# Expert 0 of a gMLP and mixture-of-experts layer: its gate and up rows laid out as k*128+p, and its first 1024 features gathered in two pieces of 512

## The reference

```python
h = x + chunked_gmlp(rmsnorm(x, norm_mix), w_in, ln_g, ln_b, w_s, b_s, w_out)
hn = rmsnorm(h, norm_ffn)
# router: the best of 4 groups, in it the best 2 of 8 experts, weights from two softmaxes
# for each expert e, over the tokens routed to it (xb: rows of hn):
y = (silu(xb @ w_gate[e]) * (xb @ w_up[e])) @ w_down[e]     # 2048 -> 512 -> 2048
out = rmsnorm(h + sum_of(weight * y), norm_final)
```

## Time and profile before

| what | before |
|---|---|
| time, median of 3 | 1198.08 us |
| time of the profiled execution | 1198.11 us |
| its span in the profile | 1196.4 us |
| TensorE matmul busy | 883.5 us, 74% |
| DMA rate, mean over the span | 385 GB/s |
| chain of waits, by engine | DMA 50%, PE 47% |
| busiest line of the chain on TensorE | L1395, the mixer, 21% |

### The profile page before, as it was taken

The page is one execution under the profiler, slowest core; times in us unless marked ns, Lnnn a source line. Parts: engine busy times, 40 slices in busy tenths (PEclk is TensorE's granted clock), DMA queues, the critical chain, the costliest instruction groups (busy, mean ns, idle before and its releaser), DMA issues.

```text
span 1196.4 us, 17569 instructions
## 1 busy us (share of the span) xinstructions
PE 883.5 (74%) x7809; PEld 501.8 (42%) x7809; DVE 381.3 (32%) x493; ACT 231.6 (19%) x390; POOL 23.0 (2%) x66
## 2 busy tenths in 40 slices
PE   9999999999984666666666666666666666666666
PEld 7888888877431222222223232222222222222222
DVE  5454866545232222222222222222222222222233
ACT  6644655444200000000000000000000000000003
POOL 1200000000200000000000000000000000000000
PEclk9999999999997777778778787878787887878788
DMA  9875567878999999999999999999999999999997
GB/s 291 327 255 193 193 225 245 302 264 315 399 424 433 429 433 429 434 431 433 433 428 433 434 431 432 434 429 434 431 433 432 430 432 435 429 431 435 426 425 334
DMA packets 47686, 460.93 MB, mean 385 GB/s; under 512 B 4025, under 2 KB 4641, under 8 KB 32289
## 3 DMA queue, kind: packets, MB, share of 16 engines
q1 hardware_dynamic: 46704, 457.19, 92.4%
q0 software_dynamic: 864, 3.21, 0.8%
q10 hardware_dynamic: 80, 0.02, 0.0%
HBM read 458.05 MB, written 2.36 MB: 385 GB/s over the span
## 4 chain that ended last, share of the span: by engine, by line
DMA 50%; PE 47%; SPq 1%; ACT 1%; DVE 1%; issue 1%; POOLq 0%; DVEq 0%
DMA high_slots<-in_e_w_up 48%; PE scattered_out L1395 21%; PE bank L1605 12%; PE bank L1703 5%; PE pair L1566 3%; PE scattered_out L1716 1%; PE pair L1574 1%; DMA out_h<-acc 1%; ACT arena L780 1%; SPq L453 0%; DMA h<-in_x 0%; DVE acc L1261 0%; SPq L469 0%; PE pair L1582 0%; PE bank L1502 0%
## 5 line engine op out<-in xcount | busy, mean ns | idle before, releaser
L1199 DVE TENSOR_TENSOR acc<-scattered_out,acc 128x2048 f32<-128x2048 f32 x58 | 132.9, 2292 | 616.9 <-PE scattered_out L1716 616.9
L1605 PE MATMUL bank<-low_slots,arena 128*32 128x256 f32 x2048 | 153.5, 455 | 147.4 <-DMA low_slots<-in_e_w_up 147.0
L1605 PE MATMUL bank<-high_slots,arena 128*32 128x256 f32 x1952 | 146.0, 457 | 138.4 <-DMA high_slots<-in_e_w_up 138.4
L1605 PEld LDWEIGHTS bank<-low_slots,arena 128*32 128x32 f32 x2048 | 83.9, 126 | 218.8 <-issue 188.8
L1605 PEld LDWEIGHTS bank<-high_slots,arena 128*32 128x32 f32 x1952 | 79.6, 127 | 206.3 <-issue 178.7
L893 DVE TENSOR_TENSOR w_lo<-w_raw,w_hi 128x1024 fp32r<-128x1024 f32 x95 | 116.5, 1226 | 113.8 <-ACT w_hi L601 113.4
L601 ACT CAST w_hi<-w_raw 128x1024 fp32r<-128x1024 f32 x95 | 99.9, 1051 | 126.8 <-PE scattered_out L1395 120.7
L1395 PE MATMUL scattered_out<-w_hi,xT_second 128*128 128x512 f32 x376 | 121.4, 394 | 0.2 <-DVE w_lo L893 0.2
L1395 PE MATMUL scattered_out<-w_hi,xT_first 128*128 128x512 f32 x376 | 120.5, 393 | 0.1
L796 ACT COPY arena<-bank 128x256 f32<-128x256 f32 x32 | 11.9, 372 | 547.9 <-PE bank L1605 547.9
L1703 PE MATMUL bank<-down_slots,arena 128*32 128x512 f32 x944 | 107.9, 596 | 0.7 <-DVE arena L1193 0.7
(11 more groups left out here) (271 smaller groups left out, 512.1 us busy)
## 6 DMA issues: line engine op xcount, KB each, us to landing
down_slots<-in_e_w_down SPq DMA_DIRECT2D x26, 4096.0 KB, 21.1
low_slots<-in_e_w_gate SPq DMA_DIRECT2D x13, 4096.0 KB, 30.2
low_slots<-in_e_w_up SPq DMA_DIRECT2D x13, 4096.0 KB, 39.3
high_slots<-in_e_w_gate SPq DMA_DIRECT2D x13, 4096.0 KB, 30.5
high_slots<-in_e_w_up SPq DMA_DIRECT2D x13, 4096.0 KB, 39.7
w_raw<-in_a_w_in SPq DMA_DIRECT2D x64, 512.0 KB, 3.7
w_raw<-in_a_w_out SPq DMA_DIRECT2D x32, 512.0 KB, 5.0
down_slots<-in_e_w_down SPq DMA_DIRECT2D x6, 2048.0 KB, 19.4
```

The costliest lines, as they stand in the source:

```text
L1199: dve.tensor_tensor(acc[:, t, :], OUT[:, :], (acc if e else h)[:, t, :], ALU.add).then_inc(acc_done, 1)
L1605: ins = pe.matmul(GU[c * CAP:(c + 1) * CAP, 0:256], rows_k, gate_columns(rows_of[c // 2][k], c % 2), start=(a == 0 and k == 0), stop=(a == ...
```

## The change

The gate and up chunks of expert 0 are read in another order: partition p holds the rows k*128 + p. A chunk of 2 MB is then 1024 pieces of 2 KB in memory, where it was 128 pieces of 16 KB. In exchange the features of block k are 128 neighbouring columns of `h`. The first half (features 0 to 1023) is gathered as two quarters of 512 features, each with its own place in PSUM, copy, transpose and scaling, and all three waits (`xe_first_ps`, `xe_first`, `xeT_first`) count to two. The second half stays whole. Its features come with a pattern of two runs of 128 columns. ScalarE's first quarter copy stands ahead of the router's exponentials, its second behind them; VectorE's first scaling stands ahead of the reduction of the exponentials. The scaling takes `g_ffn` (the columns k*128+p of `norm_ffn`) in place of `g_rows`.

```diff
-        XE_FIRST, TRX_FIRST = GU[:, 256:512], TRX[:, 256:512]
+        XE_FIRST = (GU[:, 256:384], XE[:, 256:384])
+        TRX_FIRST = (TRX[:, 256:384], TRX[:, 384:512])
...
                 w, a = (e_gate, e_up)[c % 2], c // 2
+                if e == 0:
+                    return w[0, 0].rearrange("(k p) n -> p k n", p=P)[:, 8 * a:8 * a + 8, :]
                 return w[0, e].rearrange("(p a k) n -> a p k n", a=2, k=8)[a]
...
+            act.wait_ge(xe_first_ps, 1)
+            act.copy(xe[:, 0:P], XE_FIRST[0]).then_inc(xe_first, 1)
             for i in range(2):
                 act.wait_ge(exp_in, i + 1)
                 act.activation((g_exp, e21)[i], (g_shifted, d21)[i], ACT.Exp).then_inc(exp_done, 1)
+            act.wait_ge(xe_first_ps, 2)
+            act.copy(xe[:, P:2 * P], XE_FIRST[1]).then_inc(xe_first, 1)
...
+            def scale_first(lo, hi, src, done):
+                g_first = g_ffn[:, KC * lo:KC * hi].rearrange("p (b j) -> p b j", b=hi - lo).unsqueeze(3)
+                dve.tensor_tensor(xeT[:, lo:hi, :, :], src.rearrange("p (b j c) -> p b j c", b=hi - lo, j=NQ),
+                                  g_first.to_broadcast([P, hi - lo, NQ, CAP]), ALU.mult).then_inc(done, 1)
+            dve.wait_ge(exp_in, 2)
+            dve.wait_ge(xeT_first_ps, 1)
+            scale_first(0, 1, TRX_FIRST[0], xeT_first)
             dve.wait_ge(exp_done, 2)
...
             dve.wait_ge(g_rows_in, 16)
-            scale_first(0, xeT_first_ps, TRX_FIRST, xeT_first)
+            dve.wait_ge(xeT_first_ps, 2)
+            scale_first(1, 2, TRX_FIRST[1], xeT_first)
             choose(0)
-            scale_first(1, xeT_ps, TRX, xeT_ready)
+            dve.wait_ge(xeT_ps, 1)
+            scale_first(2, 4, TRX[:, 0:2 * P], xeT_ready)
...
-                for t in range(NT):
-                    ins = gather_first(0, t)
-                ins.then_inc(xe_first_ps, 1)
+                gather_quarter(0, 0)
+                gather_quarter(0, 1).then_inc(xe_first_ps, 1)
+                gather_quarter(1, 0)
                 pe.wait_ge(xe_first, 1)
-                transpose_first(0).then_inc(xeT_first_ps, 1)
-                gather_first(1, 0)
+                transpose_quarter(0).then_inc(xeT_first_ps, 1)
+                gather_quarter(1, 1).then_inc(xe_first_ps, 1)
...
                 pe.wait_ge(xeT_first, 1)
                 gate_up_of(0, 0, rows_of, 0, 2).then_inc(gu_pair, 1)
-                gather_first(1, 1).then_inc(xe_ps, 1)
+                pe.wait_ge(xe_first, 2)
+                transpose_quarter(1).then_inc(xeT_first_ps, 1)
                 gate_up_of(0, 0, rows_of, 2, 4).then_inc(gu_pair, 1)
+                gather_second_half(0)
+                gather_second_half(1).then_inc(xe_ps, 1)
+                pe.wait_ge(xeT_first, 2)
                 gate_up_of(0, 0, rows_of, 4, 8).then_inc(gu_half, 1)
                 pe.wait_ge(xe_ready, 1)
```

More of the change, by code:

```diff
@@ L782, in copy_first @@
             def copy_first():
-                act.wait_ge(xe_first_ps, 1)
-                act.copy(xe[:, 0:2 * P], XE_FIRST[:, 0:2 * P]).then_inc(xe_first, 1)
                 act.wait_ge(xe_ps, 1)
@@ L1175, in _ @@
             g_of = g_rows[:, :].rearrange("p (b k) -> p k b", k=KC).unsqueeze(3).to_broadcast([P, KC, NQ, CAP])
[L1177 to L1184, removed]
             def scale_xeT(e):
@@ L1583, in transpose_scat, with gather_quarter, gather_second_half, transpose_quarter @@
                 ins.then_inc(scat_ps, 1)
-            def gather_first(half, t):
+            def gather_quarter(q, t):
                 pe.wait_ge((sel_first, sel_ready)[t], 1)
                 for j in range(NB):
-                    cols = h[:, t, :].rearrange("q (p a j b) -> q a j p b", a=2, j=NB, b=2)[:, half, j, :, :]
-                    ins = pe.matmul((XE_FIRST, XE)[half][j * CAP:(j + 1) * CAP, 0:2 * P], sel[:, 0, t, :], cols,
+                    col = q * NBLK + j * P
+                    ins = pe.matmul(XE_FIRST[q][j * CAP:(j + 1) * CAP, :], sel[:, 0, t, :], h[:, t, col:col + P],
                                     start=(t == 0), stop=(t == NT - 1))
                 return ins
[L1594 to L1598, removed]
-                return ins
+            def gather_second_half(t):
+                for j in range(NB):
+                    cols = h[:, t, :].rearrange("q (a j p) -> q a j p", a=KC, j=NB)[:, 2:4, j, :]
+                    ins = pe.matmul(XE[j * CAP:(j + 1) * CAP, 0:2 * P].rearrange("c (a p) -> c a p", a=2), sel[:, 0, t, :],
+                                    cols, start=(t == 0), stop=(t == NT - 1))
+                return ins
+            def transpose_quarter(q):
+                return pe.transpose(TRX_FIRST[q], xe[:, q * P:(q + 1) * P], ident[:, :])
             def gate_up_of(e, a, rows_of, lo, hi):
                 for k in range(lo, hi):
-                    rows_k = xeT[:, 2 * a + k % 2, k // 2, :] if e == 0 else xeT[:, k % KC, 2 * a + k // KC, :]
+                    rows_k = xeT[:, 2 * a + k // KC, k % KC, :] if e == 0 else xeT[:, k % KC, 2 * a + k // KC, :]
                     for c in range(NQ):
@@ L1621, in first_expert @@
                 gate_up_of(0, 0, rows_of, 0, 2).then_inc(gu_pair, 1)
-                gather_first(1, 1).then_inc(xe_ps, 1)
+                pe.wait_ge(xe_first, 2)
+                transpose_quarter(1).then_inc(xeT_first_ps, 1)
                 gate_up_of(0, 0, rows_of, 2, 4).then_inc(gu_pair, 1)
+                gather_second_half(0)
+                gather_second_half(1).then_inc(xe_ps, 1)
+                pe.wait_ge(xeT_first, 2)
                 gate_up_of(0, 0, rows_of, 4, 8).then_inc(gu_half, 1)
                 pe.wait_ge(xe_ready, 1)
-                transpose_first(1).then_inc(xeT_ps, 1)
+                for q in (2, 3):
+                    ins = pe.transpose(TRX[:, (q - 2) * P:(q - 1) * P], xe[:, q * P:(q + 1) * P], ident[:, :])
+                ins.then_inc(xeT_ps, 1)
                 transpose_scat(0)
```

## The result

The changed kernel takes 1200.78 us (median of 22 runs, 1198.05 to 1202.94), the kernel before 1198.32 us (22 runs on the same chips, 1197.15 to 1199.95). The ratio is 1.002, 95% interval 1.0014 to 1.0026: 2.5 us slower, where 0.8 us less was forecast, and outside the range that ended at 1199.6. The profiled execution of after took 1202.4 us, span 1200.3.

A forecast was written before the change was run, and what follows sets the result against it. TensorE was taken to bound the mixer and loads the experts. From 1198.1 us, 0 for the chunks and minus 0.8 for the loads gave 1197.3 us, range 1195.9 to 1199.6.

The forecast's parts named there:

- the term of the four chunks: Mixer: expert 0's re-ordered chunks load 0.5 us slower each, hidden by room behind them, so costed at nothing.
- the 0.8 us at the seam: Start of expert 0: earlier loads fill missing loading, 0.59 + 0.2 = 0.8 us gained, bounds 0 to 1.37.
- The two rooms: Mixer: delay the pieces behind chunks can take before TensorE waits, 0.85 us at chunk 1, about 1.1 estimated at chunk 0.
- ScalarE's wait behind chunk 2 is 0.5 us longer: Mixer: a sign that the forecast is right, with TensorE still busy 259.7 of 260 us.
- Rival 3: Mixer: 256 KB step halves chunk rate, 4.8 us more per chunk, 1209 us; decides from 0.85 us more; chance 0.08.
- The quarters on TensorE: Start of expert 0: gate and up start 0.83 us earlier; first two load issues 0.83 us earlier, third as good as unchanged.
- the 0.72 of hidden weight loads: First quarter's gather: 0.72 us if weight loads hide under the rounds, 1.15 if they add up; gain 0.45.
- All four terms: First quarter's gains: gather 0.45, copy 0.10, transpose 0.15, scaling 0.13 us; sum 0.83, bounds 0.02 to 1.03.
- The hole of 303 to 304 us ... closes: Start of expert 0: 0.59 us of lost loading vanishes because the first load is issued 0.83 us earlier.
- Rival 2: Start of expert 0: slow microsecond merely moves forward, or first issue gains only 0.4 us; 1198.1 to 1198.4; chance 0.25.
- The second hole: Loads at 306 to 307 us, 0.53 us lost; a quarter of 0.25 + 0.53 was counted as gain.
- a purse: Lost loading between 303 and 307 us, 1.37 us together, from which the change could pay itself.

The follow-up runs named there:

- rows_only: Kernel before with only the new row layout of chunks 0 to 3, no quarters; expert 0's result is wrong: 1200.64 us against 1198.49.
- near_2k: Kernel before with chunks 0 to 3 in 2 KB pieces 4 KB apart, not 256 KB; expert 0 computed of mismatched rows: 1201.86 us, ratio 1.0027.
- four_back: Changed kernel with each of chunks 0 to 3 issued as four DMAs of 256 pieces, one right behind the other: 1199.16 us against 1198.43.
- rows_01: Kernel before with the new rows in chunks 0 and 1 only; expert 0's output is not the reference's: 1201.0 us against 1198.43.
- after_again: Changed kernel unaltered, run once more for a second profile: 1201.44 us in one run.
- quarters_16k: Changed kernel with expert 0's chunks in 16 KB pieces again, quarters kept; expert 0's result is wrong: 1198.35 us against 1198.49.
- split: Changed kernel with each of chunks 0 to 3 as four 512 KB DMAs laid singly between w_raw pieces of the next block: 1199.02 us against 1198.49.
- split_01: Changed kernel with only chunks 0 and 1 as four 512 KB DMAs each, laid between w_raw pieces: 1198.74 us against 1198.03.

## Why the prediction was wrong, step by step

**The step that failed** is the term of the four chunks: "So 2 MB take 5.32 instead of 4.83 us, 0.5 us more for each of four chunks", and with it "I cost the chunks at nothing". They cost 2.2 to 2.5 us (`rows_only`, after); the rest of the miss of 3.3 us (2.5 slower for 0.8 faster) is the 0.8 us at the seam, below. The rate that the term used is right: after its start a chunk runs at 387 to 397 GB/s, where the row of pieces gave 394. What the term left out is the start, which the row of short DMAs did not show: a piece of `w_raw` is one DMA of 256 pieces and a chunk one of 1024. It lands the piece behind chunk 1 2.9 us later than before and the piece behind chunk 0 2.3 us later (10.6 against 8.3). The two rooms that were tested fit: 0.85 us at chunk 1 would leave 2.05 us of wait, and 1.98 was measured; at chunk 0 the estimate of 1.1 leaves 1.2, and 0.83 was measured. So the error sits in one number, the delay per chunk: 0.5 us for each of four, instead of 2.3 and 2.9 at chunks 0 and 1, about 1.0 at chunk 3 and none at chunk 2. There the sign "ScalarE's wait behind chunk 2 is 0.5 us longer" failed too: it is 1.95 us, where it was 2.00. The prediction named the point from which it decides, 0.85 us; it gave it 8 in 100.

**Rival 3** had the right side, the right place for chunks 0 and 1, and the wrong cause. The chunks come late without the step of 256 KB (`near_2k`), and with it they are hardly late when each is four DMAs (`four_back`). Its size, 4.8 us more per chunk and 12 us in all, was far off too: at most 2.9 us per piece behind, 2.5 us in all.

**The price of a wait.** Each microsecond that TensorE stood was priced at one. In the profiled execution of after 2.81 us of waits cost 4.51 us because the clock fell. I had that nowhere in the sum. It is not settled as a rule: the granted clock fell after waits of 1.98 us (after) and 2.58 us (`near_2k`), and it did not after 2.09 (`rows_01`), 1.73 (`rows_only`) and 1.62 us (`after_again`). It may be why the profiled execution of after is 1.6 us above its median, and does not make the median: `rows_only` loses 2.15 us in its median and has 2.5 us of waits with no fall.

**The quarters on TensorE were right.** Gate and up start 1.90 us after the first gather (302.74 to 304.64); 1.98 was forecast, and it was 2.81. SyncE's issues, in the rows, come 3.08, 4.39 and 7.06 us after the gather, where 3.14, 4.51 and 7.23 were forecast:

```profile
305.82 0.33 SPq L432 DMA_DIRECT2D low_slots<-in_e_w_gate  x1
...
307.13 0.33 SPq L432 DMA_DIRECT2D low_slots<-in_e_w_gate  x1
...
309.80 0.33 SPq L438 DMA_DIRECT2D low_slots<-in_e_w_gate  x1
```

The gather gives half of the 0.91 us: it takes 0.69 us, as the 0.72 of hidden weight loads said, and 1.15 is excluded. Copy, transpose and scaling give 0.11, 0.16 and 0.12 us, where 0.10, 0.15 and 0.13 were forecast. All four terms were right, so this is not luck.

**"The hole of 303 to 304 us ... closes" failed**. Rival 2 has the outcome for this half, no gain, but not the reason, since the slow microsecond neither closed nor moved with the issue. It lies 5 to 6 us after the first gather with early issues and with late ones: 197 GB/s before (303.17 to 304.17), whose issue comes 3.97 us after the gather, and also, in this order, in after, `quarters_16k` and `rows_only`:

```profile
307.74:308.74 1.00, 1.00 (x24) 0.59 (x20) 0.00 (x0) 0.37 (x1) 0.74 (x4) 1.00 0.80 242
```

```profile
303.50:304.50 1.00, 1.00 (x24) 0.62 (x20) 0.00 (x0) 0.37 (x1) 0.74 (x4) 1.00 0.89 156
```

```profile
305.97:306.97 1.00, 1.00 (x26) 0.69 (x20) 0.00 (x0) 0.00 (x0) 0.74 (x4) 1.00 0.86 246
```

The first and second of these have issues 0.9 us earlier than the third. The second hole of the trace of before, 306 to 307 us, was deeper in that one execution than in the others. The ninth microsecond after the first gather moves 180 GB/s there, 258 to 340 in the five other executions without quarters, and 356 to 414 in the six with them. So the quarters do fill something here, some 0.25 us of loading by the means (278 and 387 GB/s), which is an estimate. The end does not show it. From the first gather to the end of the span it takes 897.5 to 897.7 us in five executions without quarters (898.2 in that of before), 897.3 to 897.7 in four with them, and 898.0 and 898.2 in `split` and `split_01`. The means of six and six are 897.70 and 897.72 us: nothing of the forecast 0.8, though a tenth or two could hide in this spread.

What stays open: why one DMA of 1024 pieces starts at 200 to 280 GB/s and then runs at nearly 400, why chunk 2 with such pieces at 256 KB does not, and why loads issued 0.9 us earlier at the seam bring nothing by then. If the slow microsecond is the queue running empty, which no run here shows by itself, the runs give two bounds for how far ahead of it a load must be issued: about 1.9 us was too little (after), about 3.1 was enough (`split`). Both are read off where the stream breaks or would break, to some tenths, and `split` differs in more than the lead. The changed kernel with a clock that can't fall wasn't tried.

## What to carry over

A load's rate from the trace holds for loads of its own make. Before a 2 MB load in few long pieces is changed to 1024 short ones, price its start as well as its rate, and for each load by itself (chunk 2 shows none), and compare the sum with the room of what is queued behind it, not with the share of idle DMA time; if the room is short, issue it as several DMAs. An issue that comes earlier is worth something only if the bytes land earlier, and a hole seen in one execution is a purse only if other executions have it too.

## What was unexpected of the hardware

A single DMA of 2 MB in 1024 pieces of 2 KB landed 11.2 to 11.6 us after its issue as chunk 0, the same bytes in 128 pieces of 16 KB after 9.3 to 9.7, and in 512 pieces of 4 KB after 9.9. In the four microseconds from 44.00 us the core's loads moved 265 to 283 GB/s with it; in four DMAs of 256 such pieces it moved 350, in one DMA of 512 pieces of 4 KB 365, and in pieces of 16 KB 422 to 445. The loss is over five to seven microseconds after the issue. And it is not a property of the size alone: as chunk 2, the same kind of DMA landed after 10.2 to 10.6 us, in pieces of 16 KB after 10.0 to 10.7.
